# Two search rounds per projection chunk for the sample rows, and the bias strips' low parts in four pieces

## The chip, the cores and the metric

The kernel runs on one core of a Trainium2 chip. The metric is the device time of one execution in microseconds (us): 2262.77 us is the median of three runs of the kernel before (2259.05 to 2264.43). The profiled execution took 2260.44 us, of which its span is 2258.8 us.

## The reference, cut to what matters

One inference step of a two-layer decoder trunk runs over 512 prompt tokens and 64 sample tokens (8 requests of 8 new tokens). Layer A's mixer is sparse attention: an indexer scores all keys for every row, the `k` best are selected, and attention runs over those alone.

```
def indexer_scores(qi, wi, ki):
    dots = jnp.einsum('bthd,bsd->bths', qi, ki).astype(jnp.float32) * IDX_DIM ** -0.5
    return jnp.einsum('bths,bth->bts', jax.nn.relu(dots), wi.astype(jnp.float32) * IDX_HEADS ** -0.5)
...
    scores = jnp.where(key_pos[None, None, :] <= qpos[None, :, None], scores, NEG)
    _, sel = lax.top_k(scores, topk)          # prompt: 128 of 512 keys; sample: 256 of 2056 keys
...
    logits = jnp.einsum('btngd,btjnd->btngj', q, k_sel).astype(jnp.float32) * HEAD_DIM ** -0.5 + bias
    logits = jnp.where((dist >= 0)[:, :, None, None, :], logits, NEG)
    p = jax.nn.softmax(logits, axis=-1).astype(v_sel.dtype)
```

Both selections become additive masks in the kernel, so that the attention itself is dense. The bias depends only on the distance and the head; it is added to the logits.

## The kernel before, in words

The engines run programs of their own and meet at semaphores. TensorE is PE, VectorE DVE, ScalarE ACT, GpSimd POOL, SyncE SP. The stage around the change is mixer A of the first layer.

The input projection ("inA") has 15 chunks (`A_CHUNKS`). Chunk 0 and the next four give the indexer's keys and queries; then come ten chunks of the loop over `outs`: k, v and the eight heads' columns of q, called here by that loop's counter, k = 0 to 9. For each chunk PE runs 40 matmuls of split (high and low) fp32 weights, POOL splits the weights of a later chunk into high and low part (lines 801 and 803), and DVE takes the accumulator out of PSUM with three operations (`evacuate`, lines 2501 to 2507). PSUM holds three accumulators (`RING`), so PE may be at most three chunks ahead of DVE. The prompt attention begins on PE when the last of the ten chunks has been taken out (`pe.wait_ge(acc_evac, aend + RING)`).

Between the evacuations DVE does selection work:

- `prompt_rounds`: the 128 best keys of the prompt rows are found eight at a time, in 16 rounds of `max` and `match_replace` (line 2900) over two blocks of rows. Three rounds lie before the loop, two in each of its chunks k = 0 to 5, one in k = 6, and then `select` (line 2966) writes the two masks.
- the sample rows' threshold is found bit by bit, 32 rounds. `search(k)` is `decide(k)` and then `count(k + 1)`. `decide` (lines 2945 to 2957) waits for the count of its round (`count_set`), adds up the counts of the row's two halves after a shuffle, sets a bit of the threshold `z` and signals `seek_set`. The count that follows is made by ACT for rounds 1 to `FOUND` (7): a Sign over 1032 scores with an accumulator (line 2292). Later rounds are counted by DVE itself (line 2938). The loop over `outs` does one search in each of its last seven chunks, k = 3 to 9, so that `FOUND` rounds are found when the attention begins.

ACT's order in this stretch: copies of the new k and v rows, the DMA issues for the bias strips (`attention_loads`), count 1, count 2, the high parts of the strips (line 2309, two operations), counts 3 to 7, and then the attention. POOL computes the strips' low parts, `strip - stripH` (line 975), in two operations of 128x2048, one for each key/value head n; n = 0 waits for chunk k = 7 of PE and n = 1 for k = 8, since the low parts lie in the weight buffers of those chunks. After them POOL issues a DMA, and `block_diagonal` waits for the last evacuation.

The prompt attention has 32 units, 4 blocks of rows (i = 3, 2, 1, 0) by 8 heads g. In a unit PE adds mask, bias strips and q k into PSUM (`logits`, lines 1320 to 1329), DVE takes the negated row maximum (line 2683), ACT computes the exponentials (line 2088), PE transposes them (line 1355), ACT copies them out (lines 2119, 2123), and PE multiplies with v (line 1369). At the end of each block of rows PE spreads the reciprocals of the row sums (`row_scales`, line 1338). PE issues logits(u + 2) behind transposed(u). After the maximum of unit u DVE calls `selections(u)`: a further search for k = found + u, then, in consecutive units, the threshold (lines 3026 to 3030), the cut (lines 3035 to 3040) and the mask `maskS` (lines 3044 to 3046). With 7 rounds found before, these are in units 24, 25 and 26. The sample attention behind it needs that mask, and PE's first instruction of it (line 1467) waits for the last prompt block's output.

Of the kernel before, what the change touches and what calls it, by code (L numbers as in the profile page):

```python
# [17 lines left out]
F32 = mybir.dt.float32  # L18
# [3 lines left out]
ALU = mybir.AluOpType  # L22
# [18 lines left out]
HEADS, HD, KVH = 16, 64, 2  # L41
GRP = HEADS // KVH
# [343 lines left out]
def bass_hybrid_step(nc, io):  # L386
    ctx = ExitStack()
    with ctx:
# [186 lines left out]
        def strip_low(L, n):  # L575

            if L == "B":
                return mixers[L]["stripL"][:, n, :, :]
            return WSP[low_slots[n]].rearrange("p a c -> p (a c)").rearrange("p (g x) -> p g x", g=GRP)
# [210 lines left out]
        def _(pool):  # L790
# [180 lines left out]
            for n in range(KVH):  # L971
                m, ms = mixers["A"], MS["A"]
                pool.wait_ge(ms["strip_hi"], n + 1)
                pool.wait_ge(w_used, DONE["inA", A_CHUNKS - KVH - 1 + n])
                nc.gpsimd.tensor_tensor(strip_low("A", n), m["strip"][:, n, :, :], m["stripH"][:, n, :, :].bitcast(F32),
                                        ALU.subtract).then_inc(ms["strip_set"], 1)
            pool.dma_start(mixers["A"]["selb"].rearrange("s h b r -> s (h b r)"), io["c_selb"])\
                .then_inc(MS["A"]["selb_in"], 16)
            m, ms = mixers["A"], MS["A"]
# [46 lines left out]
        def _(pe):  # L1026
# [275 lines left out]
            def paged_prompt_attention(m, ms, aend):  # L1302
# [5 lines left out]
                def logits(u):  # L1308
                    r, i, g = units[u]
                    k0, nk = key_range("A", i)  # L1310
                    if u > 1:
                        pe.wait_ge(ms["p_set"], 2 * (u - 1))
                    if u > GRP and g == 1:
                        pe.wait_ge(ms["r_set"], 2 * r)
                    masked, w = i > 0, min(nk, 2 * P)
                    if masked:
                        pe.wait_ge(ms["pmask_set"], i)
                        pe.wait_ge(identb_in, 16)
                        for n in range(KVH):
                            mm(PS[u % 2][:, n, 0:nk], identb[:, :], m["pmask"][:, i - 1, 0:nk], start=True, stop=False)  # L1320
                    if u == 0:
                        pe.wait_ge(ms["strip_set"], KVH)
                    for n in range(KVH):
                        for k, part in enumerate((m["stripH"][:, n], strip_low("A", n))):
                            mm(PS[u % 2][:, n, nk - w:nk], m["identr"][:, :], part[:, g, 2 * P - w:2 * P],
                               start=k == 0 and not masked, stop=False)
                    for n in range(KVH):
                        h = slice(n * HD, (n + 1) * HD)
                        ins = mm(PS[u % 2][:, n, 0:nk], m["qT"][h, g, i * P:(i + 1) * P], m["kT"][h, k0:k0 + nk],
                                 start=False, stop=True)  # L1330
                    ins.then_inc(ms["qk_ps"], 1)
# [28 lines left out]
                def values(u):  # L1360
# [11 lines left out]
                    ins.then_inc(ms["pv_ps"], 1)  # L1372

                logits(0)
                logits(1)
                for u, (r, i, g) in enumerate(units):
                    more = u + 2 < len(units)
# [75 lines left out]
            def paged_sample_attention(m, ms):  # L1453
# [38 lines left out]
                def weights_transposed(b, k):  # L1492
# [3 lines left out]
                    bk = bank[PT_BANKS[(PT_GROUPS * b + k) % 2]]  # L1496
                    for c, j in enumerate(PT_TILES[k]):
                        w = P if j < NPG else NT
# [3 lines left out]
                def values(b, k):  # L1502
                    pe.wait_ge(ms["ptS_evac"], PT_GROUPS * b + k + 1)
                    if k == 0:
                        pe.wait_ge(ms["newS_set"], 1)
                        if b:
                            pe.wait_ge(ms["otS_evac"], b)
                    for j in PT_TILES[k]:
                        for n in range(KVH):
                            h, rows = slice(n * HD, (n + 1) * HD), slice(0, P if j < NPG else NT)  # L1510
                            v = m[KV_OF[b % KV_SLOTS]][:, j, KVW + n * HD:KVW + (n + 1) * HD] if j < NPG else \
                                m["vnew"][:, b, h]
                            ins = mm(bank[7][h, PV_AT], v, m["pts"][rows, j, h], start=j == PT_TILES[0][0],
                                     stop=j == NPG)
# [172 lines left out]
            m, ms = mixers["A"], MS["A"]  # L1687
# [36 lines left out]
            m, ms = mixers["B"], MS["B"]  # L1724
# [627 lines left out]
        def _(dve):  # L2352
# [272 lines left out]
            def project(name, c, outs):  # L2625

                a = FIRST_ACC[name] + c
                dve.wait_ge(w_used, DONE[name, c])
                dve.wait_ge(acc_evac, RING + a)
                for k, (rows, dst, factor) in enumerate(outs):  # L2630
                    if k:
                        steps.done(ins)
                    ins = evacuate(a, rows, dst, factor)
                ins.then_inc(acc_evac, 1)
# [95 lines left out]
            def paged_sample_attention(m, ms):  # L2730
# [13 lines left out]
                def weights(b, k):  # L2744
                    dve.wait_ge(ms["ptS_ps"], PT_GROUPS * b + k + 1)
                    if b:
                        dve.wait_ge(ms["pvS_ps"], PT_GROUPS * (b - 1) + k + 1)
                    bk, tiles = bank[PT_BANKS[(PT_GROUPS * b + k) % 2]], PT_TILES[k]
                    if tiles[0] < NPG:
# [84 lines left out]
            m, ms = mixers["A"], MS["A"]  # L2834
# [62 lines left out]
            def prompt_step(i, k):  # L2897

                top = m["mx8p"][:, i - 1, :]
                return nc.vector.max(top, scp[i]) if k % 2 == 0 else nc.vector.match_replace(scp[i], top, scp[i], TAKEN)  # L2900

            def prompt_rounds(blocks, first, count):

                done = {}
                for k in range(2 * first, 2 * (first + count)):
                    for i in blocks:
                        if i in done:
                            dve.wait_ge(dve_step, done[i])
                        steps.mark(prompt_step(i, k))
                        done[i] = steps.n  # L2910
                steps.settle()
# [7 lines left out]
            def own(k, n=0):  # L2919
                return m["count"][:, k % 2, 0, n:n + 1]  # L2920
# [7 lines left out]
            def odd_scores():  # L2928

                bits = m["rP"].rearrange("p a b c -> p (a b c)")[:, 0:SEGW].bitcast(I32)  # L2930
                steps.done(ts(bits, scs[:, :].bitcast(I32), 31, 1, ALU.logical_shift_right, ALU.bitwise_xor))
                steps.done(stt(m["scw"][:, :].bitcast(I32), scs[:, :].bitcast(I32), -2, bits, ALU.bitwise_and, ALU.bitwise_or))
# [26 lines left out]
            def search(k):  # L2959

                decide(k)
                count(k + 1)

            def select(i):

                ts(m["pmask"][:, i - 1, 0:(i + 1) * P], scp[i], TAKEN / 2, MASK, ALU.is_gt, ALU.mult)\
                    .then_inc(ms["pmask_set"], 1)

            ROUNDS = TOPK_P // 8
# [9 lines left out]
            rounds, found = 3, 0  # L2979
            steps.done(nc.vector.memset(seek[:, :], 0))  # L2980
            c = 1 + IH // 2
            outs = [(m["kT"][:, :], 1.0), (m["vT"][:, :], 1.0)] + [(m["qT"][:, g, :], HD ** -0.5) for g in range(GRP)]
            for k, (dst, factor) in enumerate(outs):
                project("inA", c + k, [(both, dst, factor)])
                if k == 2:
                    steps.done(nc.vector.tensor_copy(m["identr"][:, :], ident[:, :]))
                if k == len(outs) - FOUND - 1:
                    odd_scores()
                    ts(m["flags"][:, :], scs[:, :], z.bitcast(F32), None, ALU.is_ge, ALU.add,
                       accum_out=own(0)).then_inc(ms["count_set"], 1)  # L2990
                if k >= len(outs) - FOUND:
                    search(found)
                    found += 1
                more = min(2, ROUNDS - rounds)
                if more:
                    prompt_rounds((2, 3), rounds, more)
                    rounds += more
                    if rounds == ROUNDS:
                        select(2)
                        select(3)  # L3000

            def strips(i):

# [51 lines left out]
            m, ms = mixers["B"], MS["B"]  # L3055
# [11 lines left out]
            for g in range(GRP):  # L3067
                project("inB", 2 + g, [(both, m["qT"][:, g, :], HD ** -0.5)])
                n, step = divmod(g, 3)
                if n < KVH:  # L3070
                    strip, strip_hi, strip_lo = m["strip"][:, n, :, :], m["stripH"][:, n, :, :], strip_low("B", n)
# [41 lines left out]
SINK = 2  # L3113
STRIP_B = 2 * P + SINK
ORDER = {"A": (3, 2, 1, 0), "B": (3, 2, 1, 0)}
BITS, FOUND = 32, 7
HALF_B = NB // 2
LOGIT_GROUPS = [list(range(NB))[k:k + 3] for k in range(0, NB, 3)]

# [1 line left out]
def key_range(L, i):  # L3121

    first = 0 if L == "A" else max(0, i - 1) * P
    return first, (i + 1) * P - first
# [2 lines left out]

KT_TILES = [list(range(k, k + 4)) for k in (NPG - 4, *range(0, NPG - 4, 4))]
PT_TILES = KT_TILES + [[NPG]]
SP_PAGES, POOL_PAGES = KT_TILES[0] + KT_TILES[1], KT_TILES[2] + KT_TILES[3]  # L3130
CHUNKS = [slice(tiles[0] * P, (tiles[-1] + 1) * P) for tiles in KT_TILES]
KT_GROUPS, PT_GROUPS = len(KT_TILES), len(PT_TILES)

# [73 lines left out]
```

## Time and profile before

| | us |
|---|---|
| median of three runs | 2262.77 |
| profiled execution | 2260.44 |
| its span | 2258.8 |
| PE busy (share of the span) | 2149.0 (95%) |
| DVE busy | 1330.4 (59%) |
| POOL busy | 1211.3 (54%) |
| ACT busy | 947.2 (42%) |

Times in the trace are microseconds from the span's start. A row of the timeline gives the start, the duration, the engine, the line, the operation and its output and input; in brackets behind it, the idle time of the engine before it and what ended that. A window row gives its length and then the busy time of each engine with the number of instructions, the share of full speed that TensorE's clock was granted, the share of time that the DMA engines were busy, and what they moved in GB/s. PE's ends are modelled, so a busy PE is not one at its peak.

### The profile page before, as it was taken

The page shows a single profiled execution, that of the slowest core. Times are in us where ns is not written, and L with a number is a line of the kernel's source. Part 1 is how long each engine was busy: PE and PEld are TensorE (multiplying, and loading weights), DVE is VectorE, ACT ScalarE, POOL GpSimd, SP SyncE. Part 2 cuts the span into 40 slices and gives each one's busy share as a digit, 9 for nine tenths or more (in the row PEclk, how much of TensorE's full clock was granted, in tenths as well). Part 3 has the DMA queues.
Part 4 walks back from the last instruction along what each step waited for, and adds up shares of the span by engine and source line. Part 5 has one row for each costly group of instructions (what it writes and reads, how often), then busy time and mean ns, then how long its engine had stood idle before and what let it go on. Part 6 is the DMA issues. An engine that isn't in the chain of part 4 may idle for free.

```text
span 2258.8 us, 40965 instructions
## 1 busy us (share of the span) xinstructions
PE 2149.0 (95%) x15007; PEld 1968.3 (87%) x15007; DVE 1330.4 (59%) x2282; ACT 947.2 (42%) x1891; POOL 1211.3 (54%) x881
## 2 busy tenths in 40 slices
PE   7799999999988998999999799999999998999997
PEld 6799999958766687999999799999996797999997
DVE  5636455778886548536375754636566477455453
ACT  5524344341454425525254543525315345344343
POOL 4648576413304346758485765758451067667571
PEclk9899999999998999999999999999999799999998
DMA  5345454544103622534444253524550033435341
GB/s 129 68 120 106 122 110 96 114 87 121 42 2 114 177 47 66 103 71 97 86 92 93 51 112 66 115 64 97 116 139 20 1 75 75 104 74 114 66 104 43
DMA packets 372004, 197.68 MB, mean 88 GB/s; under 512 B 66531, under 2 KB 366284, under 8 KB 371788
## 3 DMA queue, kind: packets, MB, share of 16 engines
q1 hardware_dynamic: 356892, 172.40, 35.1%
q10 hardware_dynamic: 11552, 13.71, 2.0%
q0 software_dynamic: 3360, 8.95, 1.5%
q8 instruction: 121, 1.98, 0.4%
q14 instruction: 79, 0.65, 0.1%
HBM read 192.23 MB, written 11.64 MB: 90 GB/s over the span
## 4 chain that ended last, share of the span: by engine, by line
PE 51%; DVE 7%; ACT 2%; issue 2%; POOL 2%; DVEq 0%; POOLq 0%; ACTq 0%
PE psum L1076 8%; PE psum L1077 8%; PE psum L1078 8%; PE psum L1035 7%; PE psum L1036 4%; PE psum L1038 4%; PE psum L1034 4%; PE psum L1037 3%; DVE psum L2369 1%; DVE squares L2517 1%; PE psum L1408 1%; PE psum L1438 1%; PE psum L1424 1%; PE psum L1404 1%; DVE XS L2358 1%
## 5 line engine op out<-in xcount | busy, mean ns | idle before, releaser
L834 POOL TENSOR_TENSOR WSP<-WST,WSP 128x512 fp32r<-128x512 f32 x106 | 154.2, 1459 | 152.0 <-ACT WSP L1761 151.9
L1076 PE MATMUL psum<-XT,WSP 128*128 128x288 f32 x656 | 198.2, 302 | 8.3 <-ACT back_up L1792 7.3
L801 POOL CAST WSP<-WST 128x1024 fp32r<-128x1024 f32 (+1 forms) x41 | 45.6, 1112 | 291.7 <-PE psum L1038 254.7
L1077 PE MATMUL psum<-XT,WSP 128*128 128x288 f32 x656 | 196.2, 299 | 0.0
L1078 PE MATMUL psum<-XT,WSP 128*128 128x288 f32 x656 | 195.8, 299 | 0.0
L1076 PE MATMUL psum<-XS,WSP 128*128 128x288 f32 x552 | 164.8, 299 | 14.1 <-DVE GS L2444 14.1
L2617 DVE SCALAR_TENSOR_TENSOR X<-psum,X 128x576 f32<-128x576 f32 x64 | 48.4, 756 | 214.9 <-PE psum L1038 214.9
L1078 PE MATMUL psum<-XS,WSP 128*128 128x288 f32 x552 | 163.5, 296 | 0.0
L1077 PE MATMUL psum<-XS,WSP 128*128 128x288 f32 x552 | 163.5, 296 | 0.0
L1035 PE MATMUL psum<-GS,WSP 128*128 128x512 f32 x406 | 161.1, 397 | 0.0
L2369 DVE SCALAR_TENSOR_TENSOR psum<-S,WST 128x512 f32<-128x512 f32 x70 | 103.1, 1473 | 87.1 <-POOL S L814 85.8
L1076 PE MATMUL psum<-XT,WSX 128*128 128x288 f32 x452 | 135.2, 299 | 10.8 <-ACT shots L1948 4.7
L1035 PE MATMUL psum<-XS,WSP 128*128 128x512 f32 (+1 forms) x360 | 143.3, 398 | 0.0
L872 POOL TENSOR_TENSOR WSP<-WST,WSP 128x896 fp32r<-128x896 f32 x45 | 95.6, 2127 | 87.4 <-ACT WSP L1785 87.4
L1076 PEld LDWEIGHTS psum<-XT,WSP 128*128 128x128 f32 x656 | 126.7, 193 | 10.3 <-ACT back_up L1792 7.8
L1077 PE MATMUL psum<-XT,WSX 128*128 128x288 f32 x452 | 133.6, 296 | 0.0
L1078 PE MATMUL psum<-XT,WSX 128*128 128x288 f32 x452 | 133.5, 295 | 0.0
L834 POOL TENSOR_TENSOR WSX<-WST,WSX 128x512 fp32r<-128x512 f32 x62 | 88.0, 1422 | 74.2 <-ACT WSX L1761 74.2
L1036 PE MATMUL psum<-GS,WSP 128*128 128x320 f32 x406 | 126.7, 312 | 0.0
L1077 PEld LDWEIGHTS psum<-XT,WSP 128*128 128x128 f32 x656 | 126.3, 192 | 0.0
L1078 PEld LDWEIGHTS psum<-XT,WSP 128*128 128x128 f32 x656 | 126.0, 192 | 0.0
L1034 PE MATMUL psum<-GS,WSP 128*128 128x320 f32 x406 | 125.5, 309 | 0.0
(453 smaller groups left out, 7488.7 us busy)
## 6 DMA issues: line engine op xcount, KB each, us to landing
WST<-in_ffn_w_gate SPq DMA_DIRECT2D x148, 256.0 KB, 4.9
WST<-in_ffn_w_down SPq DMA_DIRECT2D x144, 224.0 KB, 4.2
WST<-in_ffn_w_up SPq DMA_DIRECT2D x104, 256.0 KB, 4.1
WSTX<-in_ffn_w_up SPq DMA_DIRECT2D x64, 256.0 KB, 4.4
WSTX<-in_ffn_w_down SPq DMA_DIRECT2D x48, 224.0 KB, 4.3
WST<-in_a_w_in SPq DMA_DIRECT2D x28, 256.0 KB, 4.4
WSTX<-in_ffn_w_gate SPq DMA_DIRECT2D x20, 256.0 KB, 5.0
WST<-in_b_w_in SPq DMA_DIRECT2D x20, 256.0 KB, 3.9
```

The costliest lines, as they stand in the source:

```text
L834: nc.gpsimd.tensor_tensor(by_pair(low), raw, by_pair(high).bitcast(F32), ALU.subtract).then_inc(pool_set, 1)
L872: nc.gpsimd.tensor_tensor(low, raws[RAW[key]][:, 0:DB * P], high.bitcast(F32), ALU.subtract)\
L1034: mm(front, high, x[:, 0, 0:FRONT], start=first, stop=False)
L1035: mm(split, high, x[:, :, FRONT:TOK], start=first, stop=False)
L1036: mm(front, high, x[:, 1, 0:FRONT], start=False, stop=False)
L1037: mm(back, low, x[:, 0, FRONT:TOK], start=False, stop=last)
L1038: return mm(front, low, x[:, 0, 0:FRONT], start=False, stop=last)
L1076: mm(out, high[:, c], operand(prod, 0, k), start=first and k == 0, stop=False, skip_group_check=True)
L1077: mm(out, high[:, c], operand(prod, 1, k), start=False, stop=False, skip_group_check=True)
L1078: ins = mm(out, low[:, c], operand(prod, 0, k), start=False, stop=last and k == KP - 1, skip_group_check=True)
L2369: stt(by_pair(S2), by_pair(S1), -1.0, raw_part(gate, 0), ALU.mult, ALU.subtract).then_inc(sums_set, 1)
L2617: steps.done(stt(X[:, d, :], acc(accs[d]), 0.5, X[:, d, :], ALU.mult, ALU.add))
```

## The change

The constant `FOUND` becomes 13: `SEEKING` = 7 chunks with two searches each, but one in the last. The loop's two prompt rounds of a chunk are issued one by one, and in chunks k = 3 to 8 a second search stands between them; in k = 6, behind the one round left and the two selects; in k = 7 and 8, where no round is left, directly behind the first. ACT counts rounds 1 to 13. In the attention, `selections` then has 18 searches in place of 24, with threshold, cut and mask in units 18, 19 and 20. On POOL each strip's low part is computed in four operations of 128x512 (two heads each), and PE waits for eight signals in place of two.

```
--- before.py
+++ after.py
@@ -972,8 +972,11 @@
                 m, ms = mixers["A"], MS["A"]
                 pool.wait_ge(ms["strip_hi"], n + 1)
                 pool.wait_ge(w_used, DONE["inA", A_CHUNKS - KVH - 1 + n])
-                nc.gpsimd.tensor_tensor(strip_low("A", n), m["strip"][:, n, :, :], m["stripH"][:, n, :, :].bitcast(F32),
-                                        ALU.subtract).then_inc(ms["strip_set"], 1)
+                for g in range(0, GRP, GRP // STRIP_PIECES):
+                    heads = slice(g, g + GRP // STRIP_PIECES)
+                    nc.gpsimd.tensor_tensor(strip_low("A", n)[:, heads, :], m["strip"][:, n, heads, :],
+                                            m["stripH"][:, n, heads, :].bitcast(F32), ALU.subtract)\
+                        .then_inc(ms["strip_set"], 1)
             pool.dma_start(mixers["A"]["selb"].rearrange("s h b r -> s (h b r)"), io["c_selb"])\
                 .then_inc(MS["A"]["selb_in"], 16)
             m, ms = mixers["A"], MS["A"]
@@ -1319,7 +1322,7 @@
                         for n in range(KVH):
                             mm(PS[u % 2][:, n, 0:nk], identb[:, :], m["pmask"][:, i - 1, 0:nk], start=True, stop=False)
                     if u == 0:
-                        pe.wait_ge(ms["strip_set"], KVH)
+                        pe.wait_ge(ms["strip_set"], KVH * STRIP_PIECES)
                     for n in range(KVH):
                         for k, part in enumerate((m["stripH"][:, n], strip_low("A", n))):
                             mm(PS[u % 2][:, n, nk - w:nk], m["identr"][:, :], part[:, g, 2 * P - w:2 * P],
@@ -2984,20 +2987,24 @@
                 project("inA", c + k, [(both, dst, factor)])
                 if k == 2:
                     steps.done(nc.vector.tensor_copy(m["identr"][:, :], ident[:, :]))
-                if k == len(outs) - FOUND - 1:
+                if k == len(outs) - SEEKING - 1:
                     odd_scores()
                     ts(m["flags"][:, :], scs[:, :], z.bitcast(F32), None, ALU.is_ge, ALU.add,
                        accum_out=own(0)).then_inc(ms["count_set"], 1)
-                if k >= len(outs) - FOUND:
+                if k >= len(outs) - SEEKING:
                     search(found)
                     found += 1
                 more = min(2, ROUNDS - rounds)
-                if more:
-                    prompt_rounds((2, 3), rounds, more)
-                    rounds += more
-                    if rounds == ROUNDS:
-                        select(2)
-                        select(3)
+                for n in range(2):
+                    if n < more:
+                        prompt_rounds((2, 3), rounds, 1)
+                        rounds += 1
+                        if rounds == ROUNDS:
+                            select(2)
+                            select(3)
+                    if n == 0 and len(outs) - SEEKING <= k < len(outs) - 1:
+                        search(found)
+                        found += 1
 
             def strips(i):
 
@@ -3113,7 +3120,8 @@
 SINK = 2
 STRIP_B = 2 * P + SINK
 ORDER = {"A": (3, 2, 1, 0), "B": (3, 2, 1, 0)}
-BITS, FOUND = 32, 7
+BITS, SEEKING = 32, 7
+FOUND = 2 * SEEKING - 1
 HALF_B = NB // 2
 LOGIT_GROUPS = [list(range(NB))[k:k + 3] for k in range(0, NB, 3)]
 
@@ -3127,6 +3135,7 @@
 
 KT_TILES = [list(range(k, k + 4)) for k in (NPG - 4, *range(0, NPG - 4, 4))]
 PT_TILES = KT_TILES + [[NPG]]
+STRIP_PIECES = 4
 SP_PAGES, POOL_PAGES = KT_TILES[0] + KT_TILES[1], KT_TILES[2] + KT_TILES[3]
 CHUNKS = [slice(tiles[0] * P, (tiles[-1] + 1) * P) for tiles in KT_TILES]
 KT_GROUPS, PT_GROUPS = len(KT_TILES), len(PT_TILES)
```

## Rows read from the trace of the kernel before

**Rows 1.** Busy us of PE, PEld, DVE, ACT, POOL; PEclk, DMA, GB/s, by window

```profile
538.00:586.00 48.00, 45.36 (x288) 42.53 (x287) 46.56 (x116) 12.28 (x16) 25.18 (x13) 1.00 0.60 146
...
682.00:690.00 8.00, 5.19 (x36) 3.46 (x33) 6.85 (x10) 2.59 (x13) 0.00 (x0) 0.77 0.01 2
690.00:700.00 10.00, 9.90 (x50) 6.72 (x49) 3.07 (x7) 5.65 (x23) 1.52 (x3) 0.50 0.09 25
...
712.00:812.00 100.00, 93.68 (x945) 64.51 (x945) 54.48 (x132) 40.59 (x108) 28.22 (x50) 1.00 0.51 139
```

**Rows 2.** DVE in order of time (start, us; idle), one projection chunk

```profile
554.16 0.76 DVE L2504 SCALAR_TENSOR_TENSOR qTA<-psum,rstd 128x576 f32<-128x576 f32 x1
...
555.64 0.15 DVE L2945 STREAM_SHUFFLE countA<-countA 128x1 f32<-128x1 f32 x1
...
556.07 0.16 DVE L2953 SCALAR_TENSOR_TENSOR seekA<-seekA 128x1 int32<-128x1 int32 x1
...
556.45 1.15 DVE L2900 MAX8 mx8pA<-squares 128x8 f32<-128x384 f32 x2
...
558.70 1.15 DVE L2900 MAX8 mx8pA<-squares 128x8 f32<-128x384 f32 x2
```

**Rows 3.** POOL in order of time, during the last projection chunks

```profile
558.95 2.42 POOL L803 TENSOR_TENSOR WSP<-WST,WSP 128x1024 fp32r<-128x1024 f32 x1
...
565.29 2.41 POOL L803 TENSOR_TENSOR WSP<-WST,WSP 128x1024 fp32r<-128x1024 f32 x1
570.53 4.70 POOL L975 TENSOR_TENSOR WSP<-stripA,stripHA 128x2048 fp32r<-128x2048 f32 x1 [2.83 <-PE psum L1038]
576.88 4.70 POOL L975 TENSOR_TENSOR WSP<-stripA,stripHA 128x2048 fp32r<-128x2048 f32 x1 [1.65 <-PE psum L1038]
```

**Rows 4.** DVE in order of time, operations held while POOL runs

```profile
572.63 3.14 DVE L2966 TENSOR_SCALAR pmaskA<-squares 128x384 bf16<-128x384 f32 x2
...
577.60 3.99 DVE L2953 SCALAR_TENSOR_TENSOR seekA<-seekA 128x1 int32<-128x1 int32 x1
```

**Rows 5.** ACT in order of time, one count of the sample search

```profile
583.91 1.16 ACT L2292 ACTIVATE maskSA<-scwA,seekA 128x1032 bf16<-128x1032 f32 x1 [1.05 <-DVE seekA L2953]
```

**Rows 6.** PE in order of time, its first operation of the attention

```profile
585.71 0.60 PE L1320 MATMUL psum<-pmaskA,identb 128*128 128x512 bf16 x2 [2.64 <-DVE qTA L2507]
```

**Rows 7.** PE alone by window: busy us, PEclk, DMA, a restart

```profile
512.00:516.00 4.00, 2.38 (x11) 0.54 0.00 0
516.00:520.00 4.00, 4.00 (x18) 0.61 0.00 0
```

**Rows 8.** DVE in order of time, the attention's last units

```profile
668.46 0.69 DVE L2683 TENSOR_REDUCE nmA<-psum 128x2 f32<-128x512 f32 x1
...
671.11 0.69 DVE L2683 TENSOR_REDUCE nmA<-psum 128x2 f32<-128x512 f32 x1
...
676.84 0.15 DVE L2945 STREAM_SHUFFLE countA<-countA 128x1 f32<-128x1 f32 x1
...
680.46 0.69 DVE L2662 TENSOR_TENSOR otokA<-psum,otokA 128x512 f32<-128x512 f32 x1
...
681.47 2.30 DVE L3036 TENSOR_TENSOR_SCAN squares<-scwA 128x1032 f32<-128x1032 f32 x1
...
685.38 1.28 DVE L3044 SCALAR_TENSOR_TENSOR scwA<-squares,cutA,scwA 128x1032 f32<-128x1032 f32 x1
...
688.64 0.42 DVE L2683 TENSOR_REDUCE nmA<-psum 128x2 f32<-128x256 f32 x1
...
697.70 0.42 DVE L2683 TENSOR_REDUCE nmA<-psum 128x2 f32<-128x256 f32 x1 [2.29 <-PE psum L1329]
```

**Rows 9.** PE in order of time, a gap before a unit

```profile
667.16 0.90 PE L1355 MATMUL psum<-ident,pA 128*128 128x128 f32 x4 [2.74 <-ACT pA L2088]
```

**Rows 10.** PE in order of time, first transposes of the sample attention

```profile
704.02 1.53 PE L1467 MATMUL psum<-ident,kv0A 128*128 128x128 f32 x12
```

**Rows 11.** POOL in order of time, a cast held by DVE

```profile
706.80 1.50 POOL L801 CAST WSP<-WST 128x1024 fp32r<-128x1024 f32 x1
```

More of the change, by code:

```diff
@@ L974, in _ @@
                 pool.wait_ge(w_used, DONE["inA", A_CHUNKS - KVH - 1 + n])
-                nc.gpsimd.tensor_tensor(strip_low("A", n), m["strip"][:, n, :, :], m["stripH"][:, n, :, :].bitcast(F32),
-                                        ALU.subtract).then_inc(ms["strip_set"], 1)
+                for g in range(0, GRP, GRP // STRIP_PIECES):
+                    heads = slice(g, g + GRP // STRIP_PIECES)
+                    nc.gpsimd.tensor_tensor(strip_low("A", n)[:, heads, :], m["strip"][:, n, heads, :],
+                                            m["stripH"][:, n, heads, :].bitcast(F32), ALU.subtract)\
+                        .then_inc(ms["strip_set"], 1)
             pool.dma_start(mixers["A"]["selb"].rearrange("s h b r -> s (h b r)"), io["c_selb"])\
@@ L1321, in logits @@
                     if u == 0:
-                        pe.wait_ge(ms["strip_set"], KVH)
+                        pe.wait_ge(ms["strip_set"], KVH * STRIP_PIECES)
                     for n in range(KVH):
@@ L2986, in _ @@
                     steps.done(nc.vector.tensor_copy(m["identr"][:, :], ident[:, :]))
-                if k == len(outs) - FOUND - 1:
+                if k == len(outs) - SEEKING - 1:
                     odd_scores()
@@ L2990, in _ @@
                        accum_out=own(0)).then_inc(ms["count_set"], 1)
-                if k >= len(outs) - FOUND:
+                if k >= len(outs) - SEEKING:
                     search(found)
@@ L2994, in _ @@
                 more = min(2, ROUNDS - rounds)
[L2995 to L3000, printed above, removed]
+                for n in range(2):
+                    if n < more:
+                        prompt_rounds((2, 3), rounds, 1)
+                        rounds += 1
+                        if rounds == ROUNDS:
+                            select(2)
+                            select(3)
+                    if n == 0 and len(outs) - SEEKING <= k < len(outs) - 1:
+                        search(found)
+                        found += 1
             def strips(i):
@@ L3115 @@
 ORDER = {"A": (3, 2, 1, 0), "B": (3, 2, 1, 0)}
-BITS, FOUND = 32, 7
+BITS, SEEKING = 32, 7
+FOUND = 2 * SEEKING - 1
 HALF_B = NB // 2
@@ L3129 @@
 PT_TILES = KT_TILES + [[NPG]]
+STRIP_PIECES = 4
 SP_PAGES, POOL_PAGES = KT_TILES[0] + KT_TILES[1], KT_TILES[2] + KT_TILES[3]
```

## The prediction

> **What bounds the kernel now.** I read the busy time by window first, then DVE, POOL, ACT and PE in order of time through the ten chunks and the attention. In the stage of the chunks DVE is busy 46.56 of 48 us [rows 1]; PE is nearly as busy there, but it has room for three accumulators, so the chain of DVE sets the end: PE begins the attention 2.64 us after its last matmul, released by DVE's last evacuation of q [rows 6]. What lengthens DVE's chain in this stretch lengthens the kernel. In the attention the first units are bound by PE, those of block i = 1 by both (they follow each other at 2.65 us, of which DVE has no idle time [rows 8]), and units 24 to 27 by DVE alone: threshold, cut and mask run there, PE has 5.19 busy us in 8, and its clock is granted at 0.77, then at 0.50 (1.2 GHz) to 700 [rows 1]. The sample attention behind it is PE's (93.68 of 100 us at clock 1.00 [rows 1]), so a shift at its start reaches the end of the run.
>
> **Part 1: the end of the projection.** The cost of a chunk to DVE, from its rows [rows 2]: evacuation 555.64 - 554.16 = 1.48 us, a search's `decide` 556.45 - 555.64 = 0.81, one prompt round 558.70 - 556.45 = 2.25. Six decides come in: 6 x 0.81 = 4.9 us. Issuing the two rounds one by one adds a wait for the last `match_replace` between them; no row shows it, it is between 0 and the 0.2 us of a small operation, I take 0.05 for each of six chunks, 0.3.
>
> ACT now makes 13 counts. A count is 1.16 us and an accumulator read behind it [rows 5]; from the signal, which DVE gives 0.6 us into its decide [rows 2], the answer is there about 1.35 us later. In k = 3 to 5 a prompt round of 2.25 covers it. In k = 6 a round, and then the evacuation of k = 7, do. In k = 7 and 8 the second search stands directly behind the first: DVE has 0.2 us of its own left and waits 1.15, twice: 2.3 us. Queued behind that wait on DVE are the evacuations of k = 8 and 9, and behind them PE. The strips' high parts on ACT lie between counts 2 and 3; they are 3.7 us behind a count that ends near 553.9, and count 3 then ends by 559 to 560, when DVE asks for it after a round: 0 here, up to 1 us if the strips land late.
>
> **Part 2: the holds by POOL.** DVE's one-element operation of line 2953 (two SBUF inputs) took 3.99 us in place of 0.16, until POOL's second strip operation ended, and the two selects of line 2966 took 3.14 until its first ended [rows 2 to 4]: against some 0.7 for the two selects (three and four 128 columns at the pace of an evacuation) about 6.2 us of DVE's chain are held now. In pieces of 4.70 / 4 = 1.2 us a hold is at most 1.2 long, if DVE gets its turn between pieces; the cast of 1.50 us in place of the 1.0 of its kind says that DVE does take turns [rows 11]. But the second searches move line 2953 under other POOL work. I walk DVE from the evacuation of k = 3 at 547.1: k = 4 is evacuated at 555.1 (554.16 before). Search 3 reaches line 2953 at 560.2, inside POOL's 558.95 to 561.37: 1.15 held. Search 4 at 566.0, inside 565.29 to 567.70: 1.65 held. Search 5 at 570.9, in the first strip piece: 0.85. The selects at about 579 and search 7 at 581.7 meet the second strip's pieces: 1.4 and 0.75 [rows 3]. That is 5.8 us: **the holds are about as long as before** (-0.4 us). Bounds: no hold at all, -6.2; each hold one POOL operation longer, or the 0.15 us operation of line 2957 held too, +4.
>
> The Trainium skill bears on this, "SBUF — State Buffer", section "Who interferes with whom": the pair of ports that VectorE and GpSimd share is an exclusive lock, taken by a VectorE instruction with two SBUF inputs against a GpSimd instruction that reads SBUF, and whoever issues first keeps it for the whole instruction. The trace agrees where it shows both (3.99 us for one element beside 4.70 on POOL [rows 3, 4]). By that rule the casts and subtractions of the weights hold line 2953 as well as the strips do, which speaks against the second searches of k = 4 and 5; a reading in which only long strips hold it would give the sum about 3 us less.
>
> The sum of both parts: 4.9 + 0.3 + 2.3 - 0.4 = 7.1 us later for the last evacuation, near 592.8 in place of 585.6. PE's last chunk still ends near 583, since the evacuation it needs (k = 6, near 576) is in time. So **PE idles 10 us in place of 2.6**. After a gap at 512.4 PE ran at clock 0.54 and 0.61 of full to about 518.8 [rows 7]; after a gap that long I expect 1.2 GHz for some 4.8 us. The first logits take 2 us at full clock, 4 then; the three first units are DVE's (3.18 us each for a maximum and a search), which hides the rest. Price 2.0 us; bounds 0 and 4.
>
> **Part 3: the attention.** Up to unit 17 nothing changes, as each unit has its search. Unit 18 takes decide and threshold, 680.46 - 676.84 = 3.6 us, unit 19 the cut, 3.0 (the scan alone 2.30), unit 20 the mask, 3.3 up to the next maximum at 688.64; a search with its count is 2.65 - 0.61 = 2.03 [rows 8]. These three come 1.6 + 1.0 + 1.25 = 3.85 us late against before. Units 21 to 23 have no search, but PE's own work of a unit is about 2.45 us, so they give back little: unit 22 stands 1.8 late, and unit 24 some 1.2. Then comes the gain. Before, unit 31 had its maximum at 697.70 and the sample attention began at 704.02 [rows 8, 10]. At half clock the last units followed at 2.71 us (0.42 + 2.29 idle), PE-bound; at full clock that is 1.4, and the chain maximum, exponentials, transposes, logits gives 1.6. Walked unit by unit (with the row scales behind unit 23 and the copies of ACT behind unit 26), unit 31 has its maximum 4.4 us earlier, near 693.3, and the 6.3 us behind it become 4.5: **6.2 us gained**. This needs the full clock. The gap between units 19 and 20 grows: PE waited 2.74 us before unit 20 [rows 9], and waits some 3.6 now, and the dip at 684 to 686 shows that gaps in this stretch can cost the clock. I take 1.3 us off for that and keep a gain of 4.9 (bounds: 8 gained, since 12.2 us of DVE work leave the attention; 0 where it runs at half clock as before).
>
> The mask earlier frees nobody: both queues that wait for it (SP's and POOL's pages of request 1) wait for unit 31's logits too. Eight signals in place of two cost nothing, PE is not waiting for them.
>
> **Sum:** 7.1 + 2.0 - 4.9 = +4.2 us, and 0.7 for POOL, whose memset and copies for the sample attention begin 7 us later beside the first units: 4.9 us slower. The profiled execution's 2260.44 would become 2265.3. It lies 2.3 under the median of the runs; on that median the forecast is 2267.7 us.
>
> **Rivals.**
> (a) *The clock falls in the middle of the attention* and stays low to its end, as it did from 686 to 703. What speaks for it: the longer gap before unit 20 and a DVE-bound stretch of 12 us. Against: the gap of 2.74 did not do it. Then units 20 to 23 lose about 2 us each less their slack, and the gain of part 3 is gone: +12 us, 2275.
> (b) *Faster.* The holds go: POOL's pieces leave DVE its turns and line 2953 rarely waits. The place is DVE's chain between 560 and 582, the price 6.2 us, and it decides from 5 us of holds less. With the restart near full speed: 7.1 - 5.8 + 1 - 7 = -4.7: 2258.
> (c) *No difference.* Start and tail cancel: the restart costs nothing, the tail gains its full 6.2: 7.1 - 6.2 = +0.9, 2263.7.
> (d) *The pieces work against DVE*: it does not get the pair between them, and holds last to a strip's end, +3 to +4 on the forecast: 2271.
>
> **How the numbers follow.** What can be told from no change is about 0.2%, 4.5 us. Forecast 0.35 (half of it above 4.5 us), (a) 0.15, (b) 0.14, (c) 0.22, (d) 0.14. Slower by over 0.2%: 0.19 + 0.15 + 0.13, 0.47. Faster: 0.14 and the edge of (c), 0.16. Within: 0.37. The range for 8 in 10 reaches to (b)'s edge and (a): 2258.5 to 2275. Cases of both signs are in it; the forecast's own range is 2264.5 to 2271.
>
> **What would show it.** Right: the last evacuation near 592 to 594; two idle times of DVE of 1.1 us between searches of k = 7 and 8, ended by ACT; line 2953 held at 560 and 566; a PE gap near 10 us and a low clock behind it; units 21 to 24 at 2.5 us and the last ones at 1.6 with the clock at 1.00. Wrong: the last evacuation under 589 (holds gone), or a tail of the attention still at clock 0.5.

## The result, and the profile after

The changed kernel takes 2264.93 us (median of 12 runs, 2262.21 to 2269.28), the kernel before 2261.14 (12 runs); the ratio is 1.0017, with a 95% interval of 1.0009 to 1.0024: slower by 3.8 us, between 2.0 and 5.4. The profiled spans are 2261.4 and 2258.8 us. From PE's first matmul of chunk k = 0 to its first of the output projection, the stage that holds the whole change, the traces have 292.3 us before and 294.6 after; the stretches outside it differ by -1.7 and +2.0 us, which the edit does not touch.

DVE's search operations of the changed kernel beside POOL (its row of line 2956 is line 2953 of before; compare [rows 2, 4]):

```profile
558.52 0.01 DVE L2948 LOAD_MASK_SELECT countA<-countA  x1 [0.50 <-ACT maskSA L2295]
...
558.98 0.44 DVE L2956 SCALAR_TENSOR_TENSOR seekA<-seekA 128x1 int32<-128x1 int32 x1
...
563.93 1.83 DVE L2956 SCALAR_TENSOR_TENSOR seekA<-seekA 128x1 int32<-128x1 int32 x1
...
568.79 1.11 DVE L2956 SCALAR_TENSOR_TENSOR seekA<-seekA 128x1 int32<-128x1 int32 x1
...
577.16 2.00 DVE L2969 TENSOR_SCALAR pmaskA<-squares 128x384 bf16<-128x384 f32 x2
...
579.51 0.82 DVE L2956 SCALAR_TENSOR_TENSOR seekA<-seekA 128x1 int32<-128x1 int32 x1
...
584.02 0.01 DVE L2948 LOAD_MASK_SELECT countA<-countA  x1 [1.20 <-ACT maskSA L2295]
...
588.33 0.01 DVE L2948 LOAD_MASK_SELECT countA<-countA  x1 [1.20 <-ACT maskSA L2295]
```

Line 2956 is held in searches 3, 4, 5 and 7 (counted from 0, two to a chunk from k = 3 on): 0.44, 1.83, 1.11 and 0.82 us in place of 0.16. The two selects take 2.00 (3.14 before). The idle times in brackets are DVE waiting for ACT's count: 0.50 before search 3, and 1.20 before the second searches of k = 7 and 8. POOL beside it, which answers to [rows 3]; the four strip pieces of a head are one row:

```profile
557.00 2.40 POOL L803 TENSOR_TENSOR WSP<-WST,WSP 128x1024 fp32r<-128x1024 f32 x1
...
563.34 2.40 POOL L803 TENSOR_TENSOR WSP<-WST,WSP 128x1024 fp32r<-128x1024 f32 x1
568.58 5.10 POOL L977 TENSOR_TENSOR WSP<-stripA,stripHA 128x512 fp32r<-128x512 f32 x4 [2.83 <-PE psum L1041]
574.93 5.39 POOL L977 TENSOR_TENSOR WSP<-stripA,stripHA 128x512 fp32r<-128x512 f32 x4 [1.25 <-PE psum L1041]
```

They take 5.10 and 5.39 us in place of 4.70. Where DVE is not held at all, in the PSUM kernel below, four pieces take 5.10 and 5.11 too, so 0.4 us is the price of the splitting itself; the 0.3 more of the second head stand where the selects and line 2956 took their turns. PE at the attention's start, answering to [rows 6]:

```profile
591.19 0.63 PE L1323 MATMUL psum<-pmaskA,identb 128*128 128x512 bf16 x1 [10.07 <-DVE qTA L2510]
...
592.61 2.08 PE L1332 MATMUL psum<-kTA,qTA 64*128 64x512 f32 x4
```

The gap is 10.07 us (2.64 before). PE's clock in the windows behind it, and later around unit 20 (PE alone: length, busy time, granted clock, DMA):

```profile
592.00:596.00 4.00, 4.00 (x16) 0.58 0.00 0
596.00:600.00 4.00, 4.00 (x23) 1.00 0.23 59
676.00:680.00 4.00, 3.11 (x14) 0.66 0.01 2
...
684.00:688.00 4.00, 4.00 (x57) 1.00 0.00 0
```

The clock is at 1.2 GHz for some 4 us after the restart: the first four 512-column products take 2.08 us together, the next four 1.13. It falls again in 676 to 680, behind the gap before unit 20, and is full from 684 to the end, where before it was 0.50 from 690 to 700 [rows 1]. DVE from unit 18 on, answering to [rows 8]:

```profile
664.48 0.68 DVE L2686 TENSOR_REDUCE nmA<-psum 128x2 f32<-128x512 f32 x1
...
668.72 0.69 DVE L2686 TENSOR_REDUCE nmA<-psum 128x2 f32<-128x512 f32 x1
...
672.29 2.30 DVE L3043 TENSOR_TENSOR_SCAN squares<-scwA 128x1032 f32<-128x1032 f32 x1
...
675.52 0.69 DVE L2686 TENSOR_REDUCE nmA<-psum 128x2 f32<-128x512 f32 x1 [0.29 <-DVE cutA L3047]
...
679.39 0.69 DVE L2686 TENSOR_REDUCE nmA<-psum 128x2 f32<-128x512 f32 x1
...
685.13 0.43 DVE L2686 TENSOR_REDUCE nmA<-psum 128x2 f32<-128x256 f32 x1
...
692.50 0.93 DVE L2686 TENSOR_REDUCE nmA<-psum 128x2 f32<-128x256 f32 x2
...
700.55 0.42 DVE L2686 TENSOR_REDUCE nmA<-psum 128x2 f32<-128x256 f32 x1 [1.13 <-PE psum L1332]
```

Unit 18 carries the threshold, unit 19 the cut, unit 20 the mask; units 22 to 24 follow; 692.50 is units 26 and 27, and unit 31 has its maximum at 700.55. PE's gap before unit 20 [rows 9] and its start of the sample attention [rows 10] became:

```profile
676.87 1.15 PE L1358 MATMUL psum<-ident,pA 128*128 128x128 f32 x4 [4.00 <-ACT pA L2091]
...
704.68 1.53 PE L1470 MATMUL psum<-ident,kv0A 128*128 128x128 f32 x12
```

The stage, part by part (us, from the start times in the two traces, and the end of the last evacuation):

| part | before | after | difference | predicted |
|---|---|---|---|---|
| first matmul of k = 0 to evacuation of k = 3 | 33.1 | 33.0 | -0.1 | 0 |
| to the last evacuation's end | 38.5 | 45.4 | +6.9 | +7.1 |
| to the maximum of unit 0 | 2.3 | 4.1 | +1.8 | +2.0 |
| units 0 to 17 | 66.3 | 66.3 | 0.0 | 0 (+0.7 for POOL) |
| units 17 to 24 | 22.3 | 24.1 | +1.8 | +1.2 (and 1.3 for the clock) |
| units 24 to 31 | 21.2 | 15.4 | -5.7 | -5.6 |
| to the sample attention on PE | 6.3 | 4.1 | -2.2 | -1.8 |
| sample attention | 102.3 | 102.2 | 0.0 | 0 |

### The profile page after: what moved, and what is told of

It is laid out like the page before. It is cut to its first block, busy times and chain, and to the rows that moved or that the text cites. A ratio compares the mean times of both kernels' runs of the same rounds, so it can differ in the third digit from the quotient of the medians.

```text
span 2261.4 us, 40954 instructions
## 1 busy us (share of the span) xinstructions
PE 2144.9 (95%) x14990; PEld 1966.2 (87%) x15007; DVE 1320.0 (58%) x2270; ACT 953.8 (42%) x1903; POOL 1209.8 (53%) x887
## 4 chain that ended last, share of the span: by engine, by line
PE 52%; DVE 6%; ACT 2%; issue 2%; POOL 2%; DVEq 0%; POOLq 0%; ACTq 0%
PE psum L1079 8%; PE psum L1080 8%; PE psum L1081 8%; PE psum L1038 7%; PE psum L1039 4%; PE psum L1041 4%; PE psum L1037 4%; PE psum L1040 3%; DVE squares L2520 1%; PE psum L1411 1%; PE psum L1427 1%; PE psum L1441 1%; DVE psum L2372 1%; PE psum L1407 1%; DVE XS L2361 1%
```

## The experiments

Nine kernels were timed beside the kernel before. Edits are shown against the changed kernel. "Stage" is the stretch defined above, "gap" PE's idle time before the attention, "restart" the time from the last evacuation's end to the maximum of unit 0; all from one profiled execution of each. The kernel before took 2261.42 us in the first four comparisons, 2261.59 in the next four and 2260.95 in the last.

| kernel | us, median | ratio to before, 95% interval | stage | gap | restart |
|---|---|---|---|---|---|
| before | 2261.1 | 1 | 292.3 | 2.64 | 2.3 |
| changed | 2264.93 | 1.0009 to 1.0024 | 294.6 | 10.07 | 4.1 |
| pieces alone | 2261.10 | 0.9988 to 1.0008 | 291.8 | 1.93 | 2.3 |
| searches alone | 2266.67 | 1.0019 to 1.0038 | 297.8 | 8.56 | 4.1 |
| covered searches | 2261.54 | 0.9990 to 1.0012 | 291.2 | 6.05 | 4.1 |
| operand in PSUM | 2260.46 | 0.9983 to 1.0001 | 290.1 | 4.86 | 3.8 |
| early rounds | 2258.83 | 0.9982 to 1.0003 | 288.2 | 3.81 | 3.9 |
| spread | 2255.66 | 0.9970 to 0.9987 | 285.2 | 2.02 | 2.3 |
| spread, SBUF | 2261.36 | 0.9990 to 1.0010 | 290.3 | 5.60 | 4.1 |
| eighteen rounds | 2258.30 | 0.9979 to 0.9998 | 288.6 | 1.70 | 2.3 |
| eighteen, even | 2254.48 | 0.9951 to 0.9978 | 284.1 | 1.80 | 2.3 |

**Pieces alone.**

```
-BITS, SEEKING = 32, 7
-FOUND = 2 * SEEKING - 1
+BITS, FOUND = 32, 7          # and the loop over outs of the kernel before
```

> Undo the search part, keep the pieces: the kernel before with each strip's low part in four operations. Theory (DVE's chain or PE's last chunk, whichever is later, sets the start of the attention): the two selects are held 1.3 us in place of 2.4 and line 2953 of search 4 is no longer held 3.8 us, but DVE then catches up with PE, whose last chunk ends near 583: the last evacuation comes 1.1 us earlier than in the kernel before, not 5, PE's gap there is 1.5 us in place of 2.64, and the time is 1 us less. Rival 1 (the holds are worth their length): 4 to 5 us less. Rival 2 (more signals and shorter operations cost POOL or PE something): 1 us or more slower.

No difference in the time (2261.10), 0.5 us less in the stage. DVE did catch up with PE, as its wait for PE's last chunk shows:

```profile
571.84 2.14 DVE L2969 TENSOR_SCALAR pmaskA<-squares 128x384 bf16<-128x384 f32 x2
...
578.10 0.57 DVE L2956 SCALAR_TENSOR_TENSOR seekA<-seekA 128x1 int32<-128x1 int32 x1
...
582.37 0.76 DVE L2507 SCALAR_TENSOR_TENSOR qTA<-psum,rstd 128x576 f32<-128x576 f32 x1 [3.51 <-PE psum L1041]
```

PE's gap is 1.93 us. The last evacuation ends 1.2 us earlier than before, counted from the start of the stage, and 0.7 us of that was lost behind it: the clock fell around unit 20 in this execution (0.55 from 668 to 672), where it had held in the kernel before.

**Searches alone.**

```
-STRIP_PIECES = 4
+STRIP_PIECES = 1
```

> Undo the pieces, keep the two searches per chunk. Theory: line 2956 of search 5 falls into the first strip operation and waits to its end (3.5 us in place of 0.95), the one of search 6 into the second (some 1.8 us), the selects and search 7 are no longer held (2 us less): the last evacuation comes 3.3 us later than in the changed kernel, and the time is 3 us more than the changed kernel's, 7 us above the kernel before. Rival (the holds are short whatever the size of the pieces, and the cost is only in the searches): the changed kernel's time within 1 us.

5.3 us above the kernel before and 1.7 above the changed one by the medians, where I had expected 7 and 3; the stage is 3.1 longer than the changed kernel's, with the hold where it was expected:

```profile
569.85 4.48 DVE L2956 SCALAR_TENSOR_TENSOR seekA<-seekA 128x1 int32<-128x1 int32 x1
```

```profile
569.64 4.68 POOL L977 TENSOR_TENSOR WSP<-stripA,stripHA 128x2048 fp32r<-128x2048 f32 x1 [2.83 <-PE psum L1041]
```

One element takes 4.48 us and ends with the strip operation that began before it. Here the late DVE also reached PE inside the chunks: PE stood still for 2.79 us before its last one. So the pieces are worth 3.1 us in the stage (1.7 by the medians), and since the pieces alone cost nothing, the added searches do the harm.

**Covered searches.**

```
-                    if n == 0 and len(outs) - SEEKING <= k < len(outs) - 1:
+                    if n == 0 and len(outs) - SEEKING <= k < len(outs) - SEEKING + 4:
...
-FOUND = 2 * SEEKING - 1
+FOUND = SEEKING + 4
```

> The changed kernel with the second search only in chunks k = 3 to 6, where a prompt round stands between the two; one each in k = 7, 8, 9; 11 rounds found before the attention. Theory: two decides (0.81 each) and two waits of DVE for ACT's count (1.20 each) leave the chain: last evacuation 4.0 us earlier than in the changed kernel, PE's gap 6 us; threshold, cut and mask in units 20 to 22 give 0.5 to 1 us back. Time 3 to 3.5 us less than the changed kernel, about that of the kernel before. Rival (what the changed kernel loses it loses in the attention, by the low clock around unit 20): within 1 us of the changed kernel.

2261.54: 3.4 us less than the changed kernel by the medians, 3.4 in the stage. The last evacuation came 3.8 us earlier, and the attention took 0.5 longer. The loss sat in the second searches of k = 7 and 8, not in the attention. The edit takes away two decides (1.6 us) and two waits (2.4) at once; what share the waits have is read from the rows.

**Operand in PSUM.**

```
+            def low_bits(k):
+                return bank[6][:, 0:1].bitcast(I32) if 1 <= k < FOUND - 1 else zx
...
-                    stt(z, less, bit, zx, ALU.logical_shift_left, ALU.bitwise_xor)...
+                    stt(z, less, bit, low_bits(k), ALU.logical_shift_left, ALU.bitwise_xor)...
...
+                    if k == 0:
+                        dve.wait_ge(ms["vnew_sb"], 2)
-                    steps.done(ts(zx, z, after, None, ALU.bitwise_xor))
+                    steps.done(ts(low_bits(k + 1), z, after, None, ALU.bitwise_xor))
```

> The changed kernel with one operand of line 2956 (the threshold's value for the next bit, one number a row) in a free PSUM bank during the chunks, so that the operation has one SBUF input in place of two. Nothing else moves. Theory (POOL holds operations with two SBUF inputs): no hold on line 2956 any more, 0.16 us each in place of 0.44, 1.83, 1.11 and 0.82; the selects are held as before; last evacuation 3.5 us earlier, time 3.5 us less than the changed kernel, at the level of the kernel before. Rival (any small DVE operation beside POOL is held, whatever its operands): the changed kernel's time and the same four durations.

2260.46: 4.5 us less than the changed kernel, 4.6 in the stage (3.5 expected; the selects fall between POOL's operations now and are no longer held either). The operation is line 2959 here; four times it begins inside an operation of POOL. DVE first, then POOL:

```profile
560.77 0.15 DVE L2959 SCALAR_TENSOR_TENSOR seekA<-seekA,psum 128x1 int32<-128x1 int32 x1
...
573.30 0.15 DVE L2959 SCALAR_TENSOR_TENSOR seekA<-seekA,psum 128x1 int32<-128x1 int32 x1
...
577.11 0.16 DVE L2959 SCALAR_TENSOR_TENSOR seekA<-seekA,psum 128x1 int32<-128x1 int32 x1
...
579.41 0.16 DVE L2959 SCALAR_TENSOR_TENSOR seekA<-seekA,psum 128x1 int32<-128x1 int32 x1
```

```profile
559.15 2.42 POOL L803 TENSOR_TENSOR WSP<-WST,WSP 128x1024 fp32r<-128x1024 f32 x1
...
570.72 5.10 POOL L977 TENSOR_TENSOR WSP<-stripA,stripHA 128x512 fp32r<-128x512 f32 x4 [2.83 <-PE psum L1041]
577.07 5.11 POOL L977 TENSOR_TENSOR WSP<-stripA,stripHA 128x512 fp32r<-128x512 f32 x4 [1.25 <-PE psum L1041]
```

The operation takes 0.15 to 0.16 us wherever it falls. What POOL held was the second SBUF operand of this line. This is the rule of the Trainium skill, "SBUF — State Buffer", section "Who interferes with whom", which names both conditions, two SBUF inputs on VectorE and a GpSimd instruction that reads SBUF; this run confirms the first by taking it away. The selects have one SBUF input and were held all the same (2.00 and 3.14 us in place of 0.69 here); no run varies that, so why they are held is not shown.

**Early rounds.**

```
+            prompt_rounds((2, 3), 3, 3)
-            rounds, found = 3, 0
+            rounds, found = 6, 0
```

> The changed kernel with three more prompt rounds ahead of the ten chunks, in the 8.9 us that DVE waits there for PE's first chunk; the last rounds then end in chunk k = 4. Theory: 6.9 us of rounds leave DVE's chain behind k = 3, but in k = 5 and 6 no round stands between the two searches any more, so two more waits for ACT's count come in (1.2 each) and the holds by POOL move: last evacuation 2.5 to 3.5 us earlier than in the changed kernel, time 3 us less than it, about 2261. If ACT's answer cost nothing it would be 6 us or more. Rival (PE, not DVE, is late at the attention's start): no difference from the changed kernel.

The idle time that this edit fills, ahead of the first evacuation of the ten chunks, in the kernel before (the profile names no releaser for it):

```profile
522.97 0.76 DVE L2501 TENSOR_TENSOR kTA<-psum,rstd 128x576 f32<-128x576 f32 x1 [8.89 <-issue]
```

2258.83: 6.1 us less than the changed kernel, twice what I expected. The two added waits for ACT came as forecast (four of 1.20 us in place of two), but the holds did not grow. 7.05 us of rounds less, 2.4 of these waits more, 0.35 less of the wait before search 3 and some 0.7 less of holds: 5.7, where the last evacuation came 5.9 earlier.

**Spread, and spread with both operands in SBUF.** Early rounds, and:

```
-                more = min(2, ROUNDS - rounds)
+                more = min(2 if k == 0 else 1, ROUNDS - rounds)
```

with the operand in PSUM ("spread") or as it was ("spread, SBUF").

> The combination that the theory asks for: three rounds ahead of the chunks, two in k = 0, one in each of k = 1 to 8, so that a round stands between the two searches of every chunk, and the operand of line 2956 in PSUM. A chunk costs DVE 1.48 + 0.81 + 2.35 + 0.81 = 5.45 us, less than PE's 6.35: DVE follows PE, the last evacuation ends 1.6 us behind PE's last chunk (10 in the changed kernel, 2.8 before), the clock stays at full speed at the restart. The attention keeps the changed kernel's gain of about 6 us behind unit 17. Time 7 us less than the kernel before, 2254, if the gap before unit 20 does not cost more clock. Rival (the attention's gain hangs on its late start): 3 us less than before at most.

> The same as the spread kernel, but with line 2956 reading both operands from SBUF as in the changed kernel. Theory: POOL's holds are back (up to 2.4 us in a chunk), but DVE now has 0.9 us of slack in each chunk and 2 us of lag is regained before the end; the hold of the last searches meets no POOL work. Last evacuation within 1 us of the spread kernel, time within 1.5 us of it. Rival (holds always cost their length): 4 to 5 us more than the spread kernel.

Spread: 2255.66, ratio 0.9979 (0.9970 to 0.9987): by the medians 5.9 us faster than before and 9.3 than the changed kernel. PE's first operation of the attention, and its clock in three windows of this kernel:

```profile
585.76 0.60 PE L1323 MATMUL psum<-pmaskA,identb 128*128 128x512 bf16 x2 [2.02 <-DVE qTA L2510]
```

```profile
586.00:590.00 4.00, 3.96 (x20) 1.00 0.24 48
670.00:674.00 4.00, 4.00 (x23) 0.57 0.00 0
690.00:694.00 4.00, 3.66 (x30) 1.00 0.00 0
```

The gap is back at 2 us and the restart runs at full clock. Only the gap before unit 20 still costs it (0.57). I had expected 2254, and DVE as PE's follower. One wait for ACT is left, before search 3:

```profile
560.63 0.01 DVE L2951 LOAD_MASK_SELECT countA<-countA  x1 [2.45 <-ACT maskSA L2295]
```

ACT's count for it stands behind the strips' high parts, which ACT began at 555.67 after waiting for a DMA.

With both operands in SBUF it is 2261.36, and there I was wrong: I gave the holds 1.5 us at most, and the kernel lost 5.7 by them. A chunk costs DVE 5.45 us and a hold of 1.0 or more:

```profile
573.62 1.33 DVE L2956 SCALAR_TENSOR_TENSOR seekA<-seekA 128x1 int32<-128x1 int32 x1
...
575.17 0.76 DVE L2507 SCALAR_TENSOR_TENSOR qTA<-psum,rstd 128x576 f32<-128x576 f32 x1
...
580.28 1.02 DVE L2956 SCALAR_TENSOR_TENSOR seekA<-seekA 128x1 int32<-128x1 int32 x1
...
581.53 0.76 DVE L2507 SCALAR_TENSOR_TENSOR qTA<-psum,rstd 128x576 f32<-128x576 f32 x1
```

The evacuations of k = 7 and 8 are 6.36 us apart (575.17, 581.53), PE's pace: a hold ends with POOL's operation (at 574.95 and 581.30, each within 0.02 us of the end of a strip piece), and POOL's work begins when PE ends a chunk. So DVE kept the lag that it had taken on by k = 5, and the last evacuation ended 5.5 us behind PE. Only 2.7 of the 5.1 us by which the stage is longer are the later evacuation; 1.8 are the restart, which falls to 1.2 GHz behind the gap of 5.60, and 0.7 lie in the attention. In the spread kernel the same evacuations are 5.50 us apart until DVE has caught up.

**Eighteen rounds, and the same spread evenly.** ACT counts seven (six) rounds ahead of its copies; the plan of DVE's work:

```
+            work("srsrs")                        # even: "srs"       (s: search, r: prompt round)
...
+                work(("srs", "srs", "rrr", "rrs", "srs", "srs", "srs", "srs", "s", "s")[k])
+                                                 # even: "srs" in k = 8 too
...
+            odd_scores()                         # and count 0, ahead of the chunks
```

> Eighteen rounds found before the attention: scores, count 0 and three searches ahead of the chunks in DVE's wait, seven counts of ACT ahead of its copies, operand in PSUM, rounds between all searches but in k = 8 and 9; none in k = 2, where ACT issues its DMAs. The attention has 13 searches, threshold, cut and mask in units 13 to 15. Theory: DVE stays behind PE by 1.6 to 2.5 us at the end of the chunks, and the attention from unit 16 on is free of DVE: units of i = 1 at 2.45 in place of 2.65, and the tail as in the changed kernel: 1 to 2 us less than the spread kernel, 2252 to 2253. Rival (three long units in a row cost the clock wherever they stand, and in block i = 2 more of PE's work lies behind them): not faster than the spread kernel.

> The kernel with eighteen rounds, with its work ahead of the chunks cut to two searches and one round, and the rounds spread so that chunks k = 4 to 8 have search, round, search. In the first eighteen-round kernel the first evacuation came 3.7 us late and DVE never caught up: PE stood still between chunks and ended 6.6 us later, which ate the attention's further gain of 2.8 us. Theory: without those stalls PE ends where it ended before, the last evacuation 2 to 2.5 us behind it, and both gains add up: the spread kernel's time less 2 to 3 us, 2253 to 2254. Rival (DVE is as late as in the first version, as the holds before chunk k = 4 are what delays it): 2258.

2258.30 (2252 to 2253 expected) and then 2254.48 (5 runs), ratio 0.9965 (0.9951 to 0.9978). In the first, PE's ten chunks took 75.4 us from first to last matmul in place of 68.8, which the second expectation puts down to DVE's late evacuations. The trace shows another path. PE's one gap in the chunks is before its transposes of k and v, in the first kernel and in the second:

```profile
540.75 0.48 PE L1293 MATMUL psum<-ident,kTA 128*128 128x128 f32 x1 [4.92 <-ACT kvtokA L2061]
```

```profile
539.06 0.33 PE L1293 MATMUL psum<-ident,kTA 128*128 128x128 f32 x1 [2.49 <-ACT kvtokA L2061]
```

They waited 4.92 us for ACT's copies of the new rows. ACT issues these behind its seven counts, and each count waits for a search of DVE: the seventh ran at 539.04. The gap also cost the clock, which was 0.50 from 540 to 544. The attention up to the sample part took 106.7 us from unit 0, 3.2 less than in the changed kernel. In the second, with six counts ahead of the copies, the wait was 2.49 us and the chunks took 71.6. The second is the fastest in this study, though its interval overlaps with that of the spread kernel; that it is faster than that one is not shown.

## Why the prediction was right

The forecast was 4.9 us slower; 3.8 were measured (2.0 to 5.4). By its steps:

- **The last evacuation.** 7.1 forecast, 6.9 found. The six decides are 4.9. The waits for ACT came to 2.9, since search 3 waited 0.50 for a count that stood behind the strips, a cost that I had bounded by 1 and set to 0. The holds were 3.6 for line 2956 and 1.3 for the selects, 4.9 against 6.3 before: -1.4 where I had -0.4. Of the rest, 0.5, the rounds issued one by one are 0.3: a round takes 2.36 us before another operation and 2.25 before another round. That is 0.11 in each of three chunks, where I had 0.05 in each of six; in k = 6 to 8 there was no pair of rounds to part. Four of the five holds of my walk came within 0.1 us; search 3, for which I had 1.15, came later, behind its wait, and was held 0.28. So 6.9 beside 7.1 is in part cancellation: 0.6 more of waits and 0.2 more between rounds and elsewhere, 1.0 less of holds. The PSUM operand (-4.5) takes the holds away. Covered searches (-3.4) takes away both waits of 1.20, with two of the six decides; the other four decides are read from the rows alone.
- **The restart.** 2.0 forecast, 1.8 found. In the eleven traces it is 2.3 us after gaps up to 2.64 us, and 3.8 to 4.1 after gaps of 3.81 and more.
- **The attention.** The gain behind unit 24 was 7.9 against 7.4 by the walk, the loss before it 1.8 against 1.2: 6.2 in all, as walked. The 1.3 that I kept back for the clock is the mis-sized term: the clock did fall before unit 21, but what it can have cost is within the 0.6 of units 17 to 24. Of the 7.9 us, 4.2 lie in units 24 to 27, where threshold, cut and mask had stood on DVE. The other 3.7 lie behind unit 27, where PE ran at half clock before and at full clock after. The clock fell in that tail in both traces with 7 rounds found (before, and pieces alone: 0.50 from 685 to 702), and in none of the nine with 11 or more.
- **POOL's start of the sample attention's operand**, 0.7 us: nothing is seen of it; units 0 to 17 took the same 66.3 us.

Without the 1.3 and the 0.7 the sum is 2.9 us, beside 2.4 in the stage of the two profiled executions and 3.8 (2.0 to 5.4) in the times; the timing cannot tell 2.9 from 4.9. That the measured 3.8 lies as near to 4.9 as to 2.9 speaks for neither margin; the traces show neither at its size. Of the rivals, the clock did not stay low (a), the holds did not go (b), start and tail did not cancel (c), and DVE got its turn between pieces (d). The forecast rested on this: the added work is paid in full where DVE's chain is the bound, and comes back at the attention's end, where DVE was the bound and then PE at half clock. The spread kernel shows both sides of it: with the start's cost gone, its stage is 7.1 us shorter than before, and 6.5 of that lie in the attention.

## What to carry to other kernels

Moving work to an engine that still has idle time gains little if the engine that orders it waits for each answer (1.20 us of idle time each here): put independent work between question and answer, or the round trip is paid each time. Such questions also delay what stands behind them in the asked engine's order: the copies behind seven counts cost PE 4.92 us. Before work is moved out of one stage, look for the place where its new engine really idles; here it was the 8.9 us ahead of the chunks and not the chunks. In this case a one-element operation with two SBUF operands took up to 4.48 us beside a GpSimd subtraction of 4.68; with one operand in PSUM it took 0.15 to 0.16.

## What the hardware did that was not expected

- A tensor_scalar of one element with one SBUF input (line 2960) was never held in the changed kernel: 0.15 us at 569.94, inside the second strip piece.
- An operation held by POOL got its turn at the end of POOL's current instruction, even with the next queued: line 2956 at 568.79 was done at 569.90, when the first strip piece ended, with three more to come. The four pieces of head 1, with DVE's operations in between, took 5.39 us, against 5.10 and 5.11 for four beside a DVE that was not held.
- The same gap before unit 20, 2.74 us in both traces, left the clock at full speed in the kernel before and halved it in the kernel with the pieces alone (0.60 and 0.55 from 664 to 672); in covered searches it was 2.73 us, with 0.65 from 672 to 676. So what a gap of that length cost differed between these executions.
